# Loading the second half of the first unit's weights ahead of the small vectors, in a conformer, mLSTM and mixture-of-experts block

## The reference

```
u = rms_norm(concat(meta, x), norm_mix_g)
z = u @ w_in + b_in                      # 1024 -> all projections at once
y = a * sigmoid(gate)                    # a, gate: z's first 2 x 1024 columns ("GLU")
y = depthwise_conv(y, conv_dw_w) + conv_dw_b     # 31 taps per channel
conv_out = silu(layer_norm(y)) @ conv_pw_w + conv_pw_b
mlstm_out = mlstm(q, k, v, gates of z) @ mlstm_out_w
h = x + (g_conv * conv_out + g_mlstm * mlstm_out) @ w_out
out = rms_norm(h + moe(rms_norm(h)))     # top 4 of 32 experts
```

## Time and profile before

| what | value |
|---|---|
| median of 3 runs | 1570.32 us (1569.99 to 1573.09) |
| the profiled execution | 1566.61 us |
| its span in the trace | 1564.9 us |
| PE busy | 1530.7 us (98%) |
| VectorE, POOL, ACT busy | 745.0, 528.6, 282.7 us |
| TensorE's granted clock over the span | 0.995 |

### The profile page before, as it was taken

One profiled execution on the slowest core, in us unless ns is written; L12 is line 12 of the kernel. 1 busy time (PEld: TensorE's weight loads), 2 busy tenths in 40 slices (PEclk: granted clock), 3 DMA queues, 4 the chain that ended last, 5 costly groups with the idle time before them and its releaser, 6 DMA issues.

```text
span 1564.9 us, 37659 instructions
## 1 busy us (share of the span) xinstructions
PE 1530.7 (98%) x15984; PEld 889.6 (57%) x15984; DVE 745.0 (48%) x1579; ACT 282.7 (18%) x406; POOL 528.6 (34%) x682
## 2 busy tenths in 40 slices
PE   7999999999999999999999999999999999999996
PEld 6998998877889733443444344334433443344334
DVE  4799899115233734433443344335433533343367
ACT  5333133456212300100010000001000100010001
POOL 7343433363334444322222322232222222222225
PEclk9999999999999999999999999999999999999998
DMA  7554143221175399999999999999999999999994
GB/s 221 164 167 130 56 148 121 81 81 54 58 303 216 106 333 425 424 425 426 423 423 424 424 423 425 423 419 424 422 424 422 422 424 425 423 426 424 424 422 176
DMA packets 103539, 492.24 MB, mean 315 GB/s; under 512 B 12309, under 2 KB 70569, under 8 KB 78404
## 3 DMA queue, kind: packets, MB, share of 16 engines
q1 hardware_dynamic: 83732, 463.29, 73.3%
q0 software_dynamic: 10128, 17.25, 3.0%
q10 hardware_dynamic: 9632, 11.03, 2.2%
HBM read 475.46 MB, written 24.87 MB: 320 GB/s over the span
## 4 chain that ended last, share of the span: by engine, by line
PE 87%; DMA 3%; POOL 3%; DVE 3%; issue 2%; SPq 1%; ACT 1%; POOLq 0%; DVEq 0%; ACTq 0%
PE banks L1618 38%; PE banks L1155 28%; PE banks L1647 19%; DMA xs<-u_rows,piece_now 1%; DMA code_of<-slot_table 1%; DMA stage<-in_w_in_dram 1%; DMA y_rows<-y_out,row_now 1%; POOL xs L704 0%; SPq L464 0%; POOL slot_table L722 0%; PE banks L1514 0%; POOL h_res L809 0%; DMA slot_table<-code,dest 0%; DVE h_res L2180 0%; PE banks L1387 0%
## 5 line engine op out<-in xcount | busy, mean ns | idle before, releaser
L1618 PE MATMUL banks<-w_ring,xT 128*32 128x512 f32 x6144 | 665.3, 592 | 4.0 <-DVE xT L2124 3.4
L1618 PEld LDWEIGHTS banks<-w_ring,xT 128*32 128x32 f32 x6144 | 206.7, 110 | 442.8 <-issue 438.3
L1647 PE MATMUL banks<-w_ring,actT 128*32 128x256 f32 x6144 | 337.5, 379 | 0.0
L1647 PEld LDWEIGHTS banks<-w_ring,actT 128*32 128x32 f32 x6144 | 207.1, 110 | 138.1 <-issue 18.8
L2102 DVE TENSOR_TENSOR hid<-banks,bias_now 128x512 f32<-128x512 f32 x96 | 63.9, 665 | 464.2 <-PE banks L1618 464.2
L636 POOL TENSOR_TENSOR w_lo<-stage,w_hi 128x2048 fp32r<-128x2048 f32 x38 | 175.3, 4613 | 258.0 <-ACT w_hi L862 258.0
L695 POOL TENSOR_TENSOR carrier<-carrier 1x1 f32<-1x1 f32 x161 | 32.2, 200 | 592.7 <-DVE y_out L2133 404.8
L1129 ACT ACTIVATE sig<-hid 128x256 f32<-128x256 f32 x96 | 40.0, 417 | 902.9 <-DVE hid L2103 902.9
L1155 PE MATMUL banks<-u_hi,w_hi 128*128 128x264 f32 (+1 forms) x528 | 176.7, 335 | 0.7 <-POOL w_lo L627 0.7
L1155 PE MATMUL banks<-u_hi,w_lo 128*128 128x264 f32 (+1 forms) x528 | 175.3, 332 | 0.0
L1155 PE MATMUL banks<-u_lo,w_hi 128*128 128x264 f32 (+1 forms) x528 | 174.8, 331 | 0.0
(11 more groups left out here) (307 smaller groups left out, 1451.2 us busy)
## 6 DMA issues: line engine op xcount, KB each, us to landing
w_ring<-in_expert_w_dram SPq DMA_DIRECT2D x192, 2048.0 KB, 14.9
stage<-in_w_in_dram SPq DMA_DIRECT2D x20, 1024.0 KB, 5.2
stage<-in_w_in_dram SPq DMA_DIRECT2D x16, 512.0 KB, 5.7
y_rows<-empty_row ACTq DMA_DIRECT2D x8, 1024.0 KB, 4.8
y_in<-y_rows SPq DMA_DIRECT2D x4, 2048.0 KB, 16.3
stage<-in_conv_pw_w_dram SPq DMA_DIRECT2D x4, 1024.0 KB, 5.3
stage<-in_mlstm_out_w_dram SPq DMA_DIRECT2D x4, 1024.0 KB, 5.2
stage<-in_w_out_dram SPq DMA_DIRECT2D x4, 1024.0 KB, 5.4
```

The lines of the kernel that those rows point to most:

```text
L1618: last = nc.tensor.matmul(banks[32 * g:32 * (g + 1), t].rearrange("p (c j) -> p c j", j=128), xT[:, t, k], units, start=k == 0, stop=k == ...
L1647: last = nc.tensor.matmul(banks[32 * g:32 * (g + 1), 3 + t, 0:GRP], actT[:, t, k], w2_ring[k // 4][:, k % 4, GRP * g:GRP * (g + 1)], start ...
```

## The change

One call is widened and one is taken away:

```
-            load_glu(0, (0,), first=True)
+            load_glu(0, first=True)
 
             b2 = b_in[0]
             rows = [(B_A, b2[0:V_OFF], V_OFF // P), ...
...
                     sp.dma_start(if_bias[r:r + HEADS], ...).then_inc(vecs_in, 16)
-            load_glu(0, (1,), first=True)
             sp.dma_start(vb_bc, b_in[:, V_OFF:V_OFF + D].to_broadcast([P, D])).then_inc(row_bc_in, 16)
```

## The result

The changed kernel takes 1572.36 us (median of 22 runs, 1570.06 to 1575.28) against 1570.49 us of the kernel before (22 runs, 1568.27 to 1573.60). The ratio is 1.0015 with a 95% interval of 1.0009 to 1.0021: slower by about 2 us, small but clear of zero. (The ratio is taken over the single runs; that of the two medians is 1.0012.) The forecast was no change, 1570.3.

A forecast was written before the change was run, and what follows sets the result against it. The prediction took PE (TensorE) as the bound, with 87% of the span. Its terms, -0.98 us for the second half and +1.0 us for the small loads, summed to 0.0: 1570.3 us, range 1568.0 to 1573.5.

The forecast's parts named there:

- the gap of 0.98 us: PE's stretch near 31 us lost to the late second half of the first unit's weights; removing it was forecast at -0.98 us.
- The second half lands near 19: First unit's weights: the moved second half lands near 19 instead of 25.14, ready before PE asks at 30.94; -0.98 us.
- The issue of the taps at 17.5: In the load queue, the taps were to be issued 3.7 us later than before, at 17.5 instead of 13.76.
- The landing of the small loads, forecast 25.1: Twelve small loads PE needs at 24.2 for its transposes: landing at 25.1, PE waits 0.9 us, taken as +1.0 us.
- the high end: Latest of three landing estimates for the taps: issue to landing as before, 8.4 us, so 25.9; PE waits 1.7 us.
- The 1.9 us around the transfer: Time from issue to landing, as a small load shows, added to the taps' 4.9 us on their engine.
- the low end: Earliest of three landing estimates for the taps: empty engine at 26 GB/s, landing at 24.3; PE waits 0.1 us.
- The taps spread over 16 engines: If 31 rows didn't run on one engine: taps land within a microsecond of the second half; sum -0.98 us alone.
- The second rival: Slower: PE's wait moves to the taps near 24 us; +0.7 to +4.3 us, middle +1.5, 1571.8 us; chance 0.2.
- The waiting instruction holds only PE's shift: At PE's wait for the small loads, ACT and VectorE are held too but idle anyway; only PE's shift counts.
- Carried to the end one for one: From 32 to 523 us PE never waits for weights except in one place, so its shift reaches the end unchanged.
- The size that can be told: For the whole kernel's time, a difference of 0.2% (3.1 us) is about what a measurement can tell from no change.

## Why the prediction was wrong, point by point

- *What bounds the kernel, and the gap of 0.98 us*: right. Wherever the second half was early, the marker came 0.98 us ahead of what the wait on the vectors alone would give: -0.96 to -1.03 with no wait, -0.26 with 0.71. That 0.98 is the gap of one profile; it was 1.3 in the second.
- *The second half lands near 19, ACT from 19.4, POOL done at 26.7*: right (all of it landed at 18.90, ACT 19.21, POOL 26.6).
- *The issue of the taps at 17.5*: right, 17.83. The queue let the first vector load through at 15.09 instead of 14.7.
- *The landing of the small loads, forecast 25.1*: this is the term that was mis-sized. They landed at 26.73 and 26.28, beyond even the high end of 25.9, and PE lost 2.66 and 2.21 us, not 1.0. The sum became +1.68 and +1.23 (without the clock) instead of 0.0. Of the 1.6 us between 25.1 and 26.73, 0.3 is the later issue, 0.9 the line itself (6.6 us, where I had 4.9 + 0.8), and 0.5 the two bias columns, for which I had no term: their share on this engine follows the taps (taps counted at 26.25, the columns at 26.48 and 26.73). The 1.9 us around the transfer were right: 0.9 before its first row and 0.95 behind its last. In the second profile the line was 6.1 us. I had made it too short by taking 26 GB/s over all 124 KB, although the engine's first rows come at 8 GB/s even alone. The high end was too low as well: I took the before landing as 22.2 from the tail's rate, and its last count came at 22.54. And I let the estimate lie near the low end because the weight halves would be gone from beside the taps, while the trace already had issue to landing for this very load, 8.8 us. By that, 17.5 + 8.8 = 26.3, it would have been +1.1, the right sign.
- *The taps spread over 16 engines*: the sum of that case, -0.98, was right (-1.03). The landing wasn't: 21.20, which is 2.3 us behind the second half (18.87) and not within a microsecond.
- *The second rival*, that the wait moves to the taps, is what happened, with 0.2 where it deserved more than the forecast. Its price, +0.7 to +4.3 with a middle of +1.5, held the result (+1.9 in the medians). But what took it beyond +0.7 wasn't what it names: the two issues weren't held 4.39 us each, they took 2.31 and 1.44. That its middle came so near is luck.
- *The waiting instruction holds only PE's shift*: right as to ACT and DVE, but in one of two profiles TensorE's clock fell behind the wait, which cost 1.5 us more. No term stood for that.
- *Carried to the end one for one*: right in this pair to 530 us (+1.70 at 35 us, +1.77 at 495), and against the second profile of the kernel before to the end. It leaves out the clock. Between 345 and 395 us the granted clock falls in nearly every profile, not at the same place in all, and the shift steps where it does. It was 0.89 over 345 to 360 us in the first profile of the kernel before and 1.00 throughout in the first run with the taps on 16 engines, whose shift of -1.03 at the marker is -2.57 at the output projection. In the changed kernel's second profile it fell twice (0.89 over 345 to 360 us, 0.83 over 380 to 390), and +2.70 became +3.70. So shifts of two profiles are best compared in front of 345 us. Behind 530 us the scatter of one execution is larger than the effect; the medians tell it.
- *The size that can be told*: 0.2% was too coarse. 22 runs of each told 0.15% from nothing.

## What to carry to other kernels

Before moving a load in a queue, look at how many DMA engines each load behind and ahead of it runs on: a load with a prime number of rows ran on one engine here, and everything that had to land after it on that engine waited, in either order. Splitting it into 16 and 15 rows removed both waits, the one that the change was aimed at and the one that it made. And where the trace has issue to landing of the very load that is moved, that is the estimate, before any rate worked out from a share.

## What the runs showed of the hardware

- A long line on one engine also held the issuing queue, where weight halves stood behind it. SP stood 6.14 us at the V bias in the kernel before (15.95 to 22.09), and 1.07 us in the same order with the taps on 16 engines; in the changed kernel, with no weights between the taps and the V bias, it stood 0.36 us. SP in order of time, before and after:

```profile
15.95 6.14 SPq L470 DMA_DIRECT2D vb_bc<-in_b_in_dram  x1
...
18.80 0.36 SPq L469 DMA_DIRECT2D vb_bc<-in_b_in_dram  x1
```

- With the taps between the halves SP stood 5.15 and 3.73 us at the second half's second DMA and the first vector load, which took 2.31 and 1.44 us in the changed kernel. In three profiles SP was let go 0.45 to 0.47 us behind the end of the last row of taps: 21.62 and 22.09 in the kernel before, 21.99 and 22.46 in its second profile, 20.00 and 20.45 with the taps between the halves.
- A DMA of 31 rows of 4 KB took 5.9 to 7.0 us on its one engine. Where no other transfer ran beside it, it moved only 8 GB/s from 19 to 20 us, its first whole microsecond, and 25 to 29 in those that followed.
- TensorE's granted clock fell to 0.50 (1.2 GHz) for some 3 us behind PE's wait near 25 us in one profile of the changed kernel (PE late by 2.21 us) and with the taps between the halves (late by 1.46 us), and stayed at 1.00 in the other profile of the changed kernel (late by 2.66 us) and with the broadcast out of the way (late by 1.97 us). Each fall cost 1.5 us. What decides whether it falls isn't shown.
